# Two upper-part buffers instead of four at the end of the dense block, two expert loads moved ahead, router by contiguous feature blocks, gather in two halves

## The chip, the core and the metric

The program runs on one core of one Trainium2 chip. The metric is the device time of one execution in microseconds (us), as a median over runs. TensorE is called PE, VectorE DVE, ScalarE ACT, GpSimd POOL, and SyncE SP; SP issues nearly all transfers from the chip's memory (HBM).

## What is computed

Two transformer blocks over 256 tokens of width 1024, all in float32.

```python
# first block: stick-breaking attention and a short convolution, then a mixture of experts
h = rms_norm(x, norm_mix_g); proj = h @ w_in            # 1024 x 5120
x = x + (sigmoid(g_a) * branch_a + sigmoid(g_b) * branch_b) @ w_out
h2 = rms_norm(x, norm_ffn_g)
g_logits = h2 @ w_rg + b_rg                             # 4 groups, the best one is taken
e_logits = h2 @ w_re + b_re                             # 8 experts in it, the best two
for each expert e of 32:  y += (silu(h2 @ w_gate[e]) * (h2 @ w_up[e]) * combine[:, e]) @ w_down[e]
x = x + y
# second block: attention and a spatial gating unit, layer norm, SwiGLU of width 2816, layer norm
```

The 32 experts hold 96 MiB of the weights. All of them are read, whatever the router says.

## The kernel before

**Weights.** Every weight comes in units of 1 MiB, 128 partitions by 2048 floats. There is a ring of 12 unit buffers (`ring`). The first block's dense part has 28 units (`B1_UNITS`, numbers 0 to 27), of which the first 20 (`B1_PROJ`) are `w_in`. The experts are worked in 8 quads of four experts, each with 12 units: 4 of gate, 4 of up, 4 of down.

**Dense units.** A float32 product is made of three matmuls from an upper and a lower part of each operand (`mm3`, L656 to L658). For each unit i, ACT copies the landed unit to an upper part `w_hi` (`hi(i)`, recorded as L1303) after waiting for its landing and for the release of the buffer that it writes; DVE subtracts to get the lower part (`lo(i)`, L1767), which takes the place in SBUF of the ring buffer itself; then PE multiplies and adds one to `unit_used`. There are `WB = 4` buffers of `w_hi`, so `hi(i)` waits for unit i - 4. ACT and DVE run strictly in the order in which the kernel writes their work. Units 20 to 23 are the two branch projections in "feature" form (48 matmuls), 24 to 27 are `w_out` in "token" form (24 matmuls of 512 columns). Between them DVE forms the merged activations by halves h: `merge_a(h)` (L1910), `merge_b(h)` (L1915), `merge_sum(h)` (L1921), and after ACT's upper copy `merge_lower(h)` (L1926). Its order there is

```python
merge_a(0); lo(23); merge_b(0); merge_sum(0); lo(24); merge_lower(0)
merge_a(1); merge_b(1); lo(25); merge_sum(1); merge_lower(1); lo(26); lo(27)
```

Each `merge_a` and `merge_b` frees a pair of PSUM banks (`pair_free`). A unit waits for its pair: unit 22 for `merge_a(0)`, unit 23 for `merge_b(0)`, unit 24 for `merge_a(1)`, unit 25 for `merge_b(1)`.

**Early expert loads.** Expert units 0 to 7 and 19 to 23 go to ring buffers as dense units free them (one each from `unit_used` 17 on; unit 3 goes elsewhere, below). Eleven expert units (8 to 18, `EARLY`) go to other memory as it falls free (`EARLY_AT`: place, and the `unit_used` at which it is free). Places 0 to 3 are the four `w_hi` buffers, 4 to 7 the activations of the dense part, `early_a`, `early_b` and `early_c` are elsewhere. Unit 3 has a place `early_d`. So 24 units, those of quads 0 and 1, can be loaded before the first expert matmul; the 25th needs a buffer that quad 0 has used. SP issues all of this from one queue in written order (`early_unit`, L482/L485) and waits in it.

**Router.** DVE adds the last projection to X (`x_add(t, h)`, L1943: token tile t, half h of the features). PE transposes X in 128x128 blocks (L715), taking every eighth feature, DVE or ACT copies the result to `h2T`, and PE multiplies by the router weights `wr` (`router_logits`, L848). DVE forms the choice and the place of each token (L2006 to L2031) and the selection matrix `pick` (L2037).

**A quad.** PE gathers the selected tokens with matmuls by `pick` (`gather`, L902): features 0 to 5 of 8 first, each as upper and lower part for two token tiles, 24 matmuls; features 6 and 7 come after the first gate unit. DVE scales the first four features to `heT` (`gathered(q, s)`, half 0, L2052), then the last four (half 1). PE multiplies the gate units 0 to 3 and the up units 4 to 7 (L936; units 0 and 1 need half 0, units 2 and 3 need half 1), then the down units (L956) and spreads the result to token order (L964, L966). Each unit adds one to the semaphore that SP waits for.

Of the kernel before, what the change touches and what calls it, by code (L numbers as in the profile page):

```python
# [92 lines left out]
def build(nc, consts, x, norm_mix_g, w_in, q_norm_g, k_norm_g, conv_w, w_sb_branch, w_conv_branch, w_out,  # L93
# [3 lines left out]
    with ExitStack() as ctx:  # L97
# [112 lines left out]
        bsp = gain[:, 74:82]  # L210

# [209 lines left out]
        def quad_slot(u):  # L421
# [5 lines left out]
        EARLY_AT = [(early_a, 0), (4, B1_PROJ), (5, B1_PROJ), (6, B1_UNITS - 4), (7, B1_UNITS - 4),  # L427
                    (0, B1_UNITS - 3), (1, B1_UNITS - 2), (2, B1_UNITS - 1), (3, B1_UNITS), (early_b, 0), (early_c, 0)]
        assert len(EARLY_AT) == EARLY

# [16 lines left out]
        def _(sp):  # L447
            def small(dst, src, landed):
                sp.dma_start(dst, src).then_inc(landed, 16)
# [5 lines left out]
            for i, src in enumerate(units1):  # L455
# [11 lines left out]
                if i == RING - 1:  # L467
# [6 lines left out]
                    small(wr[:, :, 0:NG], w_router_group[0].rearrange("(p k) n -> p k n", k=KD), land_small)  # L474
                    small(wr[:, :, NG:NG + NE], w_router_expert[0].rearrange("(p k) n -> p k n", k=KD), land_small)
# [30 lines left out]
            for m in range(RING):  # L506
                if m == GU - 4:
                    early_unit(GU + 1)
                    early_unit(GU + 2)
                if m == GU:  # L510
                    early_unit(GU + 3)
                    early_unit(GU + 4)
                sp.wait_ge(unit_used, B1_UNITS + m - RING + 1)
                n = ring_units[m]
                quad_unit(n // UPQ, n % UPQ, ring[:, QS[m], :], main_sems[m])
                if m >= GU:
                    early_unit(GU + 5 + m - GU)
# [133 lines left out]
        def _(pe):  # L651
# [8 lines left out]
            def parts_of(i, k):  # L660

                slot, _ = slot_of(load_of(i))
                return (w_hi[:, i % WB, :].rearrange("p (k n) -> p k n", k=k),
# [187 lines left out]

            pe.wait_ge(mgT_made, 2)
            for h in range(2):
                pe.wait_ge(lo_made, 27 + h)
                hi, lo = parts_of(26 + h, KU)
                for t in range(T):
                    tok = slice(t * P, (t + 1) * P)
                    for kk in range(KU):
                        last = mm3(ps[:, 2 * h + t, :], mgT_hi[:, KU + kk, tok], mgT_lo[:, KU + kk, tok], hi[:, kk, :],
                                   lo[:, kk, :], start=False, stop=(kk == KU - 1))  # L860
                        if (h, t, kk) == (1, 1, 1):
                            transposes(X, 4, [(x2_made, 3)], (0,))
# [4 lines left out]
            transposes(X, 4, [(x2_made, 3)], (1,))  # L867
            router_logits(0, 1)
            router_logits(1, 0)
# [47 lines left out]
            def quad_hidden(it, s, weights, landed, waits=False):  # L917
# [3 lines left out]
                gather(range(0, 6), s, waits)  # L921
# [370 lines left out]
        def _(act):  # L1292
# [21 lines left out]
            def hi(i):  # L1314
# [3 lines left out]
                if i >= WB:  # L1318
                    act.wait_ge(unit_used, i - WB + 1)
                copy(w_hi[:, i % WB, :], ring[:, slot, :]).then_inc(hi_made, 1)  # L1320
# [163 lines left out]

            for t in range(T):
                act.wait_ge(x2_made, t + 3)
                step(nc.scalar.activation(junk2[:], X[:, t, :], ACT.Square, accum_out=ss2[:, t:t + 1]))
                if t == 1:
                    act.wait_ge(turned_ps, PS_R + 3)
                    copy(h2T[:, 0:4, P:SEQ], ps[:, 6, :].rearrange("p (k n) -> p k n", k=4)).then_inc(h2a_made, 1)  # L1490
                rsqrt(y2[:, t:t + 1], ss2[:, t:t + 1], D, RMS_EPS)
                copy(xs_hi[:, t], X[:, t, :].rearrange("p (q k) -> p k q", k=KD)).then_inc(xshi_made, 1)
# [234 lines left out]
        def _(dve):  # L1727
# [35 lines left out]
            def lo(i):  # L1763
# [3 lines left out]
                tt(w_lo[slot][:], ring[:, slot, :], f32(w_hi[:, i % WB, :]), ALU.subtract).then_inc(lo_made, 1)  # L1767
# [178 lines left out]
            def h2_turned(t, j):  # L1946
                k0 = 4 * j
                dve.wait_ge(turned_ps, PS_R + 2 * t + j + 1)
# [4 lines left out]
            x_add(1, 0)  # L1953
            x_add(0, 1)
            dve.wait_ge(land_small, 16 * 8)
            h2_turned(0, 0)
            h2_turned(0, 1)
            x_add(1, 1)
            refine(y2[:, 0:1], ss2[:, 0:1], D, RMS_EPS)
            h2_turned(1, 1)  # L1960
# [3 lines left out]
            refine(y2[:, 1:2], ss2[:, 1:2], D, RMS_EPS)  # L1964
# [31 lines left out]
            step(ts(margin, margin, float(np.finfo(np.float32).tiny), None, ALU.mult))  # L1996

# [79 lines left out]

            step(tt(emask, oh2, egrp, ALU.mult))
# [3 lines left out]
            gathered(0, start0, (0,))  # L2082
# [319 lines left out]
        def _(pool):  # L2402
# [29 lines left out]
            pool.wait_ge(land_small, 16 * 8)  # L2432
# [50 lines left out]
```

## Time and profile before

| | |
|---|---|
| median of 3 runs | 716.45 us (715.24, 716.45, 718.52) |
| the profiled execution: device time | 715.94 us |
| the profiled execution: span, first to last instruction | 714.1 us |
| PE busy | 650.1 us, 91% of the span |
| DVE busy, ACT busy, POOL busy | 333.6 us, 260.5 us, 30.4 us |
| moved | 186.06 MB, 261 GB/s over the span |
| mean granted clock of TensorE | 0.959 |

A view gives starts and durations in us from the span's start. The page divides the span in 40 slices of 17.85 us; each digit is a busy share in tenths, PEclk the granted clock in tenths, GB/s what the transfers moved. A line number is that of the kernel; "x3" is a row of three like instructions in succession, with the time from the first one's start to the last one's end.

### The profile page before, as it was taken

To read this page: it belongs to the slowest core of one execution; us is meant where nothing else is said; L and a number is where in the kernel's file an instruction comes from. 1 tells how busy PE (TensorE), PEld (TensorE's weight loads), DVE (VectorE), ACT (ScalarE), POOL (GpSimd) and SP (SyncE) were. 2 spreads that over 40 slices of the span, in tenths; PEclk is the share of its full clock that TensorE was granted. 3 is DMA by queue.
4 is the path that set the end of the run, shared out by engine and by line. 5 is a ranking of instruction groups with operands and counts; after the bars stand their busy time and mean duration, and the time that the engine had idled before them with its cause. 6 is when DMAs were issued, how large, how long until landed. Compare 5 with 4: busy or idle time off the path is not lost.

```text
span 714.1 us, 11499 instructions
## 1 busy us (share of the span) xinstructions
PE 650.1 (91%) x4957; PEld 530.3 (74%) x4957; DVE 333.6 (47%) x409; ACT 260.5 (36%) x323; POOL 30.4 (4%) x19
## 2 busy tenths in 40 slices
PE   6999999999989999669787899999899999999995
PEld 5789999999856555244432587778689999999994
DVE  5864437566461222001010465759846444444446
ACT  5747454453411111101010453766236443333330
POOL 0610000000100000000000000330000000000000
PEclk9999999999999999957977899999999999999998
DMA  8979334787999999999999998335445556750001
GB/s 316 408 205 357 121 130 167 253 304 262 406 382 406 386 406 408 409 406 406 409 409 407 389 407 315 116 106 189 143 152 177 177 182 191 259 193 0 0 1 60
DMA packets 108491, 186.06 MB, mean 261 GB/s; under 512 B 9632, under 2 KB 33312, under 8 KB 108448
## 3 DMA queue, kind: packets, MB, share of 16 engines
q1 hardware_dynamic: 108160, 185.36, 70.8%
q8 instruction: 34, 0.56, 0.3%
q10 hardware_dynamic: 288, 0.07, 0.0%
q14 instruction: 9, 0.07, 0.0%
HBM read 184.37 MB, written 1.05 MB: 260 GB/s over the span
## 4 chain that ended last, share of the span: by engine, by line
PE 74%; DMA 11%; DVE 10%; ACT 2%; issue 2%; SPq 1%; DVEq 0%; ACTq 0%
PE ps L656 18%; PE ps L658 17%; PE ps L657 17%; PE ps L936 6%; DMA ring<-in_w_up_e 5%; DMA ring<-in_w_down_e 4%; PE ps L956 4%; PE ps L902 3%; DVE w_lo L1767 3%; DMA ring<-in_w_in 1%; PE ps L964 1%; PE ps L966 1%; PE ps L785 1%; ACT w_hi L1303 1%; DVE X L2314 1%
## 5 line engine op out<-in xcount | busy, mean ns | idle before, releaser
L1303 ACT ACTIVATE w_hi<-ring 128x2048 fp32r<-128x2048 f32 (+1 forms) x77 | 141.1, 1859 | 5.4 <-DMA ring<-in_w_in 5.2
L1767 DVE TENSOR_TENSOR w_lo<-ring,w_hi 128x2048 fp32r<-128x2048 f32 x49 | 114.8, 2354 | 52.2 <-ACT w_hi L1303 52.1
L656 PE MATMUL ps<-xT_hi,w_hi 128*128 128x256 f32 x320 | 90.6, 283 | 0.0
L658 PE MATMUL ps<-xT_hi,w_lo 128*128 128x256 f32 x320 | 90.6, 283 | 0.0
L657 PE MATMUL ps<-xT_lo,w_hi 128*128 128x256 f32 x320 | 90.6, 283 | 0.0
L936 PE MATMUL ps<-ring,heT 128*32 128x256 f32 x880 | 59.0, 409 | 15.6 <-DMA ring<-in_w_up_e 11.0
L656 PE MATMUL ps<-hT_hi,w_hi 128*128 128x256 f32 x224 | 64.0, 286 | 0.0
L657 PE MATMUL ps<-hT_lo,w_hi 128*128 128x256 f32 x224 | 63.4, 283 | 0.0
L658 PE MATMUL ps<-hT_hi,w_lo 128*128 128x256 f32 x224 | 63.3, 283 | 0.0
L657 PEld LDWEIGHTS ps<-xT_lo,w_hi 128*128 128x128 f32 x320 | 61.4, 192 | 0.4
L656 PEld LDWEIGHTS ps<-xT_hi,w_hi 128*128 128x128 f32 x320 | 61.4, 192 | 0.4
L658 PEld LDWEIGHTS ps<-xT_hi,w_lo 128*128 128x128 f32 x320 | 61.4, 192 | 0.0
L2345 DVE TENSOR_TENSOR w_lo<-ring,w_hi 128x2048 fp32r<-128x2048 f32 x24 | 54.3, 2286 | 8.9 <-ACT w_hi L1303 8.9
L936 PEld LDWEIGHTS ps<-ring,heT 128*32 128x32 f32 x880 | 29.1, 115 | 35.9 <-DMA ring<-in_w_up_e 16.2
L656 PE MATMUL ps<-w_hi,xT_hi 128*128 128x512 f32 (+1 forms) x112 | 43.1, 385 | 5.5 <-DVE xT_lo L2161 2.6
L656 PEld LDWEIGHTS ps<-hT_hi,w_hi 128*128 128x128 f32 x224 | 43.0, 192 | 0.2 <-issue 0.2
L657 PEld LDWEIGHTS ps<-hT_lo,w_hi 128*128 128x128 f32 x224 | 43.0, 192 | 0.0
L658 PEld LDWEIGHTS ps<-hT_hi,w_lo 128*128 128x128 f32 x224 | 42.9, 192 | 0.0
L658 PE MATMUL ps<-w_hi,xT_lo 128*128 128x512 f32 (+1 forms) x112 | 41.7, 372 | 0.0
L657 PE MATMUL ps<-w_lo,xT_hi 128*128 128x512 f32 (+1 forms) x112 | 41.5, 370 | 0.0
L956 PE MATMUL ps<-ring,actT 128*32 128x512 f32 x208 | 30.2, 702 | 8.5 <-DMA ring<-in_w_down_e 5.6
L2052 DVE TENSOR_TENSOR heT<-ps,gain 128x512 f32<-128x512 f32 x16 | 11.1, 691 | 53.2 <-PE ps L902 53.0
(315 smaller groups left out, 1128.5 us busy)
## 6 DMA issues: line engine op xcount, KB each, us to landing
ring<-in_w_in SPq DMA_DIRECT2D x29, 1024.0 KB, 13.7
ring<-in_w_up_e SPq DMA_DIRECT2D x28, 1024.0 KB, 13.4
ring<-in_w_gate_e SPq DMA_DIRECT2D x27, 1024.0 KB, 12.4
ring<-in_w_down_e SPq DMA_DIRECT2D x26, 1024.0 KB, 13.4
ring<-in_w_gate SPq DMA_DIRECT2D x11, 1024.0 KB, 5.4
ring<-in_w_up SPq DMA_DIRECT2D x11, 1024.0 KB, 5.5
ring<-in_w_down SPq DMA_DIRECT2D x11, 1024.0 KB, 5.0
ring<-in_w_out SPq DMA_DIRECT2D x8, 1024.0 KB, 9.8
```

The source lines that it names most:

```text
L656: mm(o, a_hi, b_hi, start=start, stop=False, skip_group_check=True)
L657: mm(o, a_hi, b_lo, start=False, stop=False, skip_group_check=True)
L658: return mm(o, a_lo, b_hi, start=False, stop=stop, skip_group_check=True)
L785: mm(o[:, 0:SEQ], negu, stick[:, h, 0:SEQ], start=False, stop=False, skip_group_check=True)
L902: last = mm(ps[:, 6 + k // 4, (k % 4) * P:(k % 4 + 1) * P], xs_lo(t, k) if part else xs_hi[:, t, k, :], pick[:, t, :], start=(part == 0 an ...
L936: last = mm(ps[32 * j:32 * j + 32, 4 + u // 4, 0:FE], heT[:, k, 32 * j:32 * j + 32], wv[:, j // 2, j % 2, kk, :], start=(k == 0), stop=(k ...
L956: last = mm(ps[32 * j:32 * j + 32, 6 + h, :], actT[:, k, 32 * j:32 * j + 32], wv[:, j, :], start=(k == 0), stop=(k == KF - 1))
L964: mm(ps[:, 2 * t + h, :], pickT[:, t, :], ysb_hi[:, cols], start=False, stop=False, skip_group_check=True)
L1303: return nc.scalar.activation(o, i, ACT.Copy)
L1767: tt(w_lo[slot][:], ring[:, slot, :], f32(w_hi[:, i % WB, :]), ALU.subtract).then_inc(lo_made, 1)
L2052: tt(heT[:, 4 * b:4 * b + 4, :], ps[:, 6 + b, :].rearrange("p (k n) -> p k n", k=4), bc(g2[:, 4 * b:4 * b + 4], P), ALU.mult).then_inc(s[" ...
L2345: tt(w_lo[slot][:], ring[:, slot, :], f32(w_hi[:, i % WB, :]), ALU.subtract).then_inc(lo_made, 1)
```

## The change

Units 20 to 27 use only `w_hi` buffers 0 and 1, in turn, so that buffers 2 and 3 take expert loads from `unit_used` 20 on. Four early loads are then issued from `unit_used` 20 on, in place of two (the third and fourth ahead of the next two ring loads); with `unit_used` 25 and 26 there is none any more, where one each was. The router's features go in contiguous blocks of 128 (k p) in place of every eighth, so its transposes can be done by halves of X as each half is added; its weights and a second copy of the gain (`g2_block`) are loaded in that layout. The first quad's `heT` half 0 is moved ahead of four small DVE steps, and the first gather call (features 0 to 5) becomes two (0 to 3, then 4 and 5).

```diff
-        EARLY_AT = [(early_a, 0), (4, B1_PROJ), (5, B1_PROJ), (6, B1_UNITS - 4), (7, B1_UNITS - 4),
-                    (0, B1_UNITS - 3), (1, B1_UNITS - 2), (2, B1_UNITS - 1), (3, B1_UNITS), (early_b, 0), (early_c, 0)]
+        EARLY_AT = [(early_a, 0), (2, B1_PROJ), (3, B1_PROJ), (4, B1_PROJ), (5, B1_PROJ),
+                    (6, B1_UNITS - 4), (7, B1_UNITS - 4), (0, B1_UNITS - 1), (1, B1_UNITS), (early_b, 0), (early_c, 0)]
+        def upper_of(i):
+            return i % 2 if B1_PROJ <= i < B1_UNITS else i % WB
+        upper_user = {}
+        for i in range(S1 + B2_PRE + 2):
+            upper_user[i] = max((j for j in range(i) if upper_of(j) == upper_of(i)), default=None)
...
-                    small(wr[:, :, 0:NG], w_router_group[0].rearrange("(p k) n -> p k n", k=KD), land_small)
-                    small(wr[:, :, NG:NG + NE], w_router_expert[0].rearrange("(p k) n -> p k n", k=KD), land_small)
+                    with nc.allow_non_contiguous_dma(reason="router weights by blocks of features"):
+                        small(g2_block, norm_ffn_g[0].rearrange("(k p) -> p k", p=P), land_small)
+                        small(wr[:, :, 0:NG], w_router_group[0].rearrange("(k p) n -> p k n", p=P), land_small)
+                        small(wr[:, :, NG:NG + NE], w_router_expert[0].rearrange("(k p) n -> p k n", p=P), land_small)
...
             for m in range(RING):
-                if m == GU - 4:
-                    early_unit(GU + 1)
-                    early_unit(GU + 2)
-                if m == GU:
-                    early_unit(GU + 3)
-                    early_unit(GU + 4)
+                for k in {GU - 4: (1, 2), GU - 3: (3,), GU - 2: (4,), GU: (5, 6)}.get(m, ()):
+                    early_unit(GU + k)
                 sp.wait_ge(unit_used, B1_UNITS + m - RING + 1)
...
-                if m >= GU:
+                if m >= GU + 2:
                     early_unit(GU + 5 + m - GU)
...
+            def router_turn(t, j):
+                pe.wait_ge(x2_made, 1 + t + 2 * j)
+                for k in range(4 * j, 4 * j + 4):
+                    ins = nc.tensor.transpose(ps[:, 4 + 2 * t + j, (k % 4) * P:(k % 4 + 1) * P],
+                                              X[:, t, k * P:(k + 1) * P], ident)
+                ins.then_inc(turned_ps, 1)
...
+                        if (h, t, kk) == (1, 0, 2):
+                            router_turn(0, 0)
+                            router_turn(1, 0)
                         if (h, t, kk) == (1, 1, 1):
-                            transposes(X, 4, [(x2_made, 3)], (0,))
+                            router_turn(0, 1)
...
             router_logits(0, 0)
-            transposes(X, 4, [(x2_made, 3)], (1,))
             router_logits(0, 1)
+            router_turn(1, 1)
             router_logits(1, 0)
             router_logits(1, 1).then_inc(logit_ps, 1)
...
-                gather(range(0, 6), s, waits)
+                gather(range(0, KD // 2), s, waits)
+                gather(range(KD // 2, 6), s, waits)
...
             def hi(i):
-                if i >= WB:
-                    act.wait_ge(unit_used, i - WB + 1)
-                copy(w_hi[:, i % WB, :], ring[:, slot, :]).then_inc(hi_made, 1)
+                before = upper_user.get(i, i - WB)
+                if before is not None:
+                    act.wait_ge(unit_used, before + 1)
+                copy(w_hi[:, upper_of(i), :], ring[:, slot, :]).then_inc(hi_made, 1)
...
+            act.wait_ge(turned_ps, PS_R + 2)
+            copy(h2T[:, 0:4, P:SEQ], ps[:, 6, :].rearrange("p (k n) -> p k n", k=4)).then_inc(h2a_made, 1)
             for t in range(T):
                 act.wait_ge(x2_made, t + 3)
                 step(nc.scalar.activation(junk2[:], X[:, t, :], ACT.Square, accum_out=ss2[:, t:t + 1]))
-                if t == 1:
-                    act.wait_ge(turned_ps, PS_R + 3)
-                    copy(h2T[:, 0:4, P:SEQ], ps[:, 6, :].rearrange("p (k n) -> p k n", k=4)).then_inc(h2a_made, 1)
                 rsqrt(y2[:, t:t + 1], ss2[:, t:t + 1], D, RMS_EPS)
-                copy(xs_hi[:, t], X[:, t, :].rearrange("p (q k) -> p k q", k=KD)).then_inc(xshi_made, 1)
+                if t == 0:
+                    xs_upper(0, slice(0, KD // 2))
+            xs_upper(0, slice(KD // 2, KD)).then_inc(xshi_made, 1)
+            xs_upper(1, slice(0, KD)).then_inc(xshi_made, 1)
...
             x_add(0, 0)
             x_add(1, 0)
+            h2_turned(0, 0)
             x_add(0, 1)
-            dve.wait_ge(land_small, 16 * 8)
-            h2_turned(0, 0)
             h2_turned(0, 1)
+            dve.wait_ge(land_small, 16 * 9)
+            refine(y2[:, 0:1], ss2[:, 0:1], D, RMS_EPS)
             x_add(1, 1)
-            refine(y2[:, 0:1], ss2[:, 0:1], D, RMS_EPS)
-            h2_turned(1, 1)
...
+            gathered(0, start0, (0,))
             step(tt(emask, oh2, egrp, ALU.mult))
             ts(oh1, rank, 0.0, None, ALU.is_equal)
             step(red(m2, emask, AX, ALU.add))
             tt(eexp, m2, m1, ALU.subtract).then_inc(gdiff_made, 1)
-            gathered(0, start0, (0,))
```

`h2_turned(1, 1)` and the second `refine` move behind two small DVE steps that need neither. PE's, ACT's and DVE's indices into `w_hi` all go through `upper_of`.

## Rows read from the trace of the kernel before

**Rows 1.** The page's 40 slices: PE, granted clock, GB/s.

```profile
PE   6999999999989999669787899999899999999995
...
PEclk9999999999999999957977899999999999999998
...
GB/s 316 408 205 357 121 130 167 253 304 262 406 382 406 386 406 408 409 406 406 409 409 407 389 407 315 116 106 189 143 152 177 177 182 191 259 193 0 0 1 60
```

**Rows 2.** The chain that ended last, 240 to 470 us: start, duration, what.

```profile
371.05 16.32 DMA ring<-in_w_up_e
387.40 1.98 PE ps L936 x16
```

**Rows 3.** Stretches: busy time (and instructions) by engine, granted clock, DMA share, GB/s.

```profile
165.00:170.00 5.00, 5.00 (x39) 4.79 (x38) 0.95 (x1) 0.00 (x0) 0.00 (x0) 1.00 0.50 191
...
175.00:180.00 5.00, 5.00 (x24) 4.14 (x23) 4.42 (x3) 3.31 (x2) 0.00 (x0) 1.00 1.05 408
...
232.50:235.00 2.50, 1.81 (x16) 0.74 (x18) 0.91 (x3) 0.66 (x2) 0.00 (x0) 1.00 1.00 333
```

**Rows 4.** SP's queue in order of time: start, duration, line, transfer, count.

```profile
146.41 1.05 SPq L485 DMA_DIRECT2D early<-in_w_down_e  x2
151.76 17.65 SPq L482 DMA_DIRECT2D ring<-in_w_up_e  x4
169.45 0.51 SPq L485 DMA_DIRECT2D early<-in_w_down_e  x1
...
174.92 0.51 SPq L482 DMA_DIRECT2D early<-in_w_gate_e  x1
...
191.76 0.37 SPq L485 DMA_DIRECT2D ring<-in_w_down_e  x1
...
202.92 0.37 SPq L482 DMA_DIRECT2D early_c<-in_w_up_e  x1
...
218.96 4.93 SPq L485 DMA_DIRECT2D early<-in_w_down_e  x2
232.41 3.02 SPq L485 DMA_DIRECT2D ring<-in_w_down_e  x2
```

**Rows 5.** ACT, DVE and PE around unit 24, in order of time.

```profile
150.14 5.53 ACT L1303 ACTIVATE w_hi<-ring 128x2048 fp32r<-128x2048 f32 x3
...
160.09 2.29 DVE L1767 TENSOR_TENSOR w_lo<-ring,w_hi 128x2048 fp32r<-128x2048 f32 x1
162.30 1.22 DVE L1926 TENSOR_TENSOR mgT_lo<-ga,mgT_hi 128x1024 fp32r<-128x1024 f32 x1
163.43 1.22 DVE L1910 TENSOR_TENSOR ga<-ps,ga 128x1024 f32<-128x1024 f32 x1
...
168.85 0.40 PE L656 MATMUL ps<-w_hi,mgT_hi 128*128 128x512 f32 x1
```

**Rows 6.** PE from the router's transposes of tile 1 to its last logits.

```profile
192.51 1.16 PE L715 MATMUL ps<-cst,X 128*128 128x128 f32 x8
193.51 2.79 PE L848 MATMUL ps<-wr,h2T 128*128 128x36 f32 x24
```

**Rows 7.** DVE around quad 0's start; the chain at quad 1's start.

```profile
201.70 1.13 DVE L2076 TENSOR_TENSOR xs_lo1b<-X,xs_hi 128x512 fp32r<-128x512 f32 x1
...
203.51 0.69 DVE L2052 TENSOR_TENSOR heT<-ps,gain 128x512 f32<-128x512 f32 x1
...
206.45 0.69 DVE L2052 TENSOR_TENSOR heT<-ps,gain 128x512 f32<-128x512 f32 x1
...
223.31 0.60 issue
```

**Rows 8.** SP's small loads at 33 us, the loads behind them, ACT's upper copy of unit 12.

```profile
32.78 6.12 SPq L449 DMA_DIRECT2D gain<-in_b_spatial  x1
...
44.81 17.93 SPq L460 DMA_DIRECT2D ring<-in_w_in  x8
...
84.11 1.90 ACT L1303 ACTIVATE w_hi<-ring 128x2048 fp32r<-128x2048 f32 x1
```

More of the change, by code:

```diff
@@ L210, in build @@
         bsp = gain[:, 74:82]
+        g2_block = gain[:, 82:90]
         ss1, y1, n1 = st[:, 0:2], st[:, 2:4], st[:, 4:10]
@@ L662, in parts_of @@
                 slot, _ = slot_of(load_of(i))
-                return (w_hi[:, i % WB, :].rearrange("p (k n) -> p k n", k=k),
+                return (w_hi[:, upper_of(i), :].rearrange("p (k n) -> p k n", k=k),
                         w_lo[slot][:].rearrange("p (k n) -> p k n", k=k))
@@ L1482, in _, with xs_upper @@
             hi(27)
+            act.wait_ge(turned_ps, PS_R + 2)
+            copy(h2T[:, 0:4, P:SEQ], ps[:, 6, :].rearrange("p (k n) -> p k n", k=4)).then_inc(h2a_made, 1)
+            def xs_upper(t, ks):
+                return copy(xs_hi[:, t, ks], X[:, t, :].rearrange("p (q k) -> p k q", k=KD)[:, ks])
             for t in range(T):
@@ L1766, in lo @@
                 dve.wait_ge(hi_made, i + 1)
-                tt(w_lo[slot][:], ring[:, slot, :], f32(w_hi[:, i % WB, :]), ALU.subtract).then_inc(lo_made, 1)
+                tt(w_lo[slot][:], ring[:, slot, :], f32(w_hi[:, upper_of(i), :]), ALU.subtract).then_inc(lo_made, 1)
             def bc(ap, n):
@@ L1947, in h2_turned @@
                 k0 = 4 * j
-                dve.wait_ge(turned_ps, PS_R + 2 * t + j + 1)
+                dve.wait_ge(turned_ps, PS_R + t + 2 * j + 1)
                 nc.vector.tensor_copy(h2T[:, k0:k0 + 4, t * P:(t + 1) * P],
@@ L1963, in _ @@
                 nc.vector.engine_nop().then_inc(pair_free[h], 1)
-            refine(y2[:, 1:2], ss2[:, 1:2], D, RMS_EPS)
             pos = [0]
@@ L1996, in _ @@
             step(ts(margin, margin, float(np.finfo(np.float32).tiny), None, ALU.mult))
+            h2_turned(1, 1)
+            refine(y2[:, 1:2], ss2[:, 1:2], D, RMS_EPS)
             def beats(out, vals, n):
@@ L2428, in _ @@
                    ).then_inc(normed_split, 1)
-            pool.wait_ge(land_small, 16 * 8)
-            tt(wr[:], wr[:], g2.unsqueeze(2).to_broadcast([P, KD, NG + NE]), ALU.mult).then_inc(wr_made, 1)
+            pool.wait_ge(land_small, 16 * 9)
+            tt(wr[:], wr[:], g2_block.unsqueeze(2).to_broadcast([P, KD, NG + NE]), ALU.mult).then_inc(wr_made, 1)
             def xs_lower(t, parts):
```

## The prediction

> **What bounds the kernel now.** I began with the page's slices [rows 1]. PE is at nine tenths nearly everywhere but in the 17th to the 23rd slice (286 to 411 us), and exactly there the transfers stand at 389 to 409 GB/s. From the 11th to the 24th they never fall below 382. So three regimes follow each other: a dense part paced by PE, an expert part paced by the weight stream, and a second block paced by PE again, where the rate is 106 to 259 GB/s, with nothing to load at the very end. The chain of waits gives the seam: PE waits 16.32 us for an expert unit's landing and starts at 387.40 [rows 2]; what follows in the chain is computation. What decides the end is when the stream delivers the last expert units, and that is the moment from which it runs without a hole, plus the bytes left. One unit is 1.0486 MB, 2.57 us at 408 GB/s.
>
> Then the stretches and SP's queue, to see where the stream is short of bytes and where of buffers. At 165 to 170 us it moves 191 GB/s, at 175 to 180 it moves 408 [rows 3]. SP issues ring loads as PE finishes dense units: four between 151.76 and 169.41, that is at 151.76, 157.5, 163.3 and 169.04, 5.76 us apart, for `unit_used` 21 to 24 [rows 4]. Two early loads follow at 169.45, and from 174.51 on each of three ring loads brings one early load along (that of 174.92 is shown), so nine loads are issued from 169.04 until just before 191.76. At 2.57 us that is 23.1 us of work in 22.7 us: just busy. The last free buffers are filled by the loads issued at 218.96 to 223.89; then SP issues nothing until 232.41, when quad 1 gives back a ring buffer, and the rate at 232.5 to 235 falls to 333 GB/s [rows 3, 4]. **This is the point on which I build:** at 232 us the stream has run out of buffers, not of time. Whatever moves earlier before it is lost in this gap, unless PE gives the buffer back earlier.
>
> **The two loads moved ahead.** No buffer is added; 24 units can still be in place before quad 0. Of those issued at 174.92 and about 5.4 us later, two transfers (5.14 us of stream) go into the hole of 152 to 169 us. Issued from 169.04 to 191.76 are then seven loads, 18.0 us of work: the stream idles nearly 5 us there. After 191.76 the same loads follow as before. What can reach 232 us is no more than the backlog that stood at 191.76: 23.1 - 22.7 = 0.4 us from below, one load of 2.57 us from above, since the time from issue to first byte is open. I take 0.7 us, near the lower end, up to there, and 0 beyond it, because the gap before 232.41 takes it.
>
> **Two upper buffers.** `hi(i)` now waits for unit i - 2. Durations are those of [rows 5]: three `hi` in 5.53 us, 1.84 us apart and 1.90 long (the single one in [rows 8]), `lo` 2.29 (2.21 to the next start), merges 1.22 (1.13). By the release times of [rows 4]: `hi(22)` starts at 151.76, `lo(22)` ends at 156.0, `merge_a(0)` at 157.1; unit 22 would start at 157.3, no loss. `hi(23)` starts at 157.5, `lo(23)` ends 161.7, `merge_b(0)` 162.9; unit 23 would start at 163.1, no loss. `hi(24)` waits for unit 22, released at 163.3, and ends at 165.2. `lo(24)` runs to 167.5, where before it ran at 160.09. Behind it in DVE's order stand `merge_lower(0)`, to 168.7, and `merge_a(1)`, to 169.8. Unit 24 needs all three, the last for its PSUM pair; before, it started at 168.85. **PE stalls 1.0 us there.** Next: `lo(25)` ends about 173.2 against unit 25's start, now near 175.3; `hi(26)` may start at 175.5 and `lo(26)` ends at 179.7 against 180.7; `lo(27)` ends near 185.1 against 186.2. None of these is late. Bounds: 0 (if the stall were covered) to 1.2 us (one more merge).
>
> **Small loads.** The three new small loads take 1024 pieces each (g2 in 4 bytes, the weights in rows of 16 and 128 bytes). The nearest row is the load of `b_spatial`, also 1024 pieces of 4 bytes: 6.12 us on SP's queue [rows 8]. From below they cost what single rows cost now, under 1 us each; from above 3 x 6.12 = 18.4 us. Queued behind them are the ring loads from 44.81 on, unit 12 first, which ACT needs at 84.11. Even 18.4 us later it is issued at 63.2, 21 us ahead. The cost is 0; with that cover gone it would be up to 18 us. The Trainium skill ("DMA: Bandwidth & Descriptors", Rules for kernel authors) says that a strided last dimension lowers to one descriptor per element, and advises against it. It speaks against this edit; the row of `b_spatial` agrees that such a load is slow, and by either the sum stays the same, since the cover is wider than the price.
>
> **Router.** PE is the bound from the last dense matmul to the logits: 8 transposes, then 24 router instructions with no idle between [rows 6]. The change moves transposes but makes as many (16): four more fall inside unit 27 (0.1 us each, from 8 in about 1.0 us, so it ends 0.4 us later) and four fewer behind it. Net 0; I take -0.1 us for the shorter wait on the last copy. ACT's copies to `xs_hi` end about 1 us later, POOL's lower part about 3 us later, at 198.5; the gather needs it after 202, so both are covered by 3 us.
>
> **Gather.** `heT` half 0 becomes possible after 16 matmuls, not 22. At 0.11 us each that is 0.7 us earlier. In quad 0 DVE is free only when `xs_lo1b` is done, 201.70 + 1.13 = 202.83, so half 0 moves from 203.51 to 202.8: -0.7. But the four small steps now stand behind it, ACT's exponential waits for them, and all DVE work up to half 1 goes with it: half 1, before at 206.45, comes 0.2 us later [rows 7]. Gate unit 2 needs half 1 at 207.1 already. So the gain of units 0 and 1 ends in a wait for half 1: quad 0 as a whole +0.2 us. Bounds: -0.7 (half 1 not late) to +0.3. In quad 1 the idle 0.60 us before the first gate matmul [rows 7] goes, because the 8 matmuls of features 4 and 5 run beside DVE's 0.69: -0.6 us, bounds -0.6 and 0.
>
> **Sum.** The release that comes at 232.41 shifts by +1.0 (stall) - 0.1 (router) + 0.2 (quad 0) - 0.6 (quad 1) = +0.5 us. The stream restarts 0.5 us later, runs at the same rate over the same bytes, and hands over at 387.9 in place of 387.4; behind it nothing changes. The profiled execution has 715.94 us, 1.8 above its span of 714.1, and lies 0.5 under the median of the three runs. 715.94 + 0.5 = 716.4; set to the median, 716.45 + 0.5, about 716.9. Ends of the terms: 0 - 0.1 - 0.7 - 0.6 = -1.4 and 1.2 + 0.3 = +1.5; with the runs' own spread (715.24 to 718.52) the likeliest case has the range 715 to 718.6.
>
> **Rivals.** *No stall* (chance 0.17). If `merge_a(1)` or `lo(24)` is not late, the sum is -0.5 or, with half 1 in time, down to -1.4: 715.1 to 716.0. For it: the slack in the dense part is large elsewhere. Against it: DVE's written order.
>
> *The two loads count in full* (0.13). If the gap at 232 is not a shortage of buffers but a side effect of the full queue, so that bytes moved before stay moved, the stream ends 2 x 2.57 = 5.1 us earlier: 711.3. For it: 400 GB/s from 171 us on, so every byte in it seems to cost. Against it: SP's 8.5 us without an issue. The Trainium skill (same page and section) advises to issue a transfer early, so that it overlaps computation. By that rule alone this rival would be the result; the rule doesn't ask whether a buffer is free later on.
>
> *Slower* (0.10). The two buffers put release, `hi` and `lo` in series: 0 + 1.9 + 2.3 = 4.2 us in units of 5.45 to 5.76. If in units 24 to 27 each `lo` also had a 1.22 us merge in front of it that my order of events puts elsewhere, three more stalls of 1.0 to 1.2 follow: +0.5 + 3.4 = +3.9, 720.4. It decides once the stalls pass 4.1 us in all; each passes one to one to the release at 232.41. Against it: 1.0 us or more of slack at each of units 25 to 27 above.
>
> **Chances.** Forecast 0.60, no stall 0.17, both within 0.5%, which is 3.6 us and about what a measurement of this kernel can tell from no change; full gain 0.13, faster; slower 0.10. That gives faster 0.13, same 0.77, slower 0.10. The range of 8 in 10 holds the first two with their spread and reaches toward both others: 712.5 to 719.5.
>
> **What would show it.** Right: one PE idle of about 1.0 us before the first matmul of unit 24, ended by L1910 of DVE; GB/s higher in 152 to 169 us and well under 400 in 175 to 192; SP's first ring load after quad 1's release at 232 to 233.5; the 0.60 us idle gone in each quad; quad 0 waiting for half 1 of `heT`; the stretch behind the last expert landing as long as before. Wrong: the stream's rate not falling around 233, or the landing at 387.4 moved by over 2 us; several idles in units 24 to 27; or a different spell of lowered clock behind 387 us, which I haven't priced.

## The result, and the profile after

The changed kernel takes 718.51 us (median of 12 runs, 715.44 to 723.84), the kernel before beside it 717.07 (12 runs, 714.03 to 719.03). The ratio is 1.0042 with an interval of 1.0022 to 1.0063, so some 3.0 us slower (1.6 to 4.5). Forecast were 0.5 us more. A second measurement of the same two kernels (e10, below) gave 1.0020 [0.9996, 1.0044], 1.4 us (-0.3 to 3.2). All medians and ratios are of fast runs; one run of the kernel before, taken beside e13, was slow (1264.35 us) and is not counted. The profiled execution took 720.63 us with a span of 718.8 and a mean granted clock of 0.946, against 0.959 before.

The page's slices answer to [rows 1]:

```profile
PE   6999999999999999769777898999899999999995
...
PEclk9999999999999999768887699999999999999998
...
GB/s 316 408 158 393 127 132 169 251 337 346 271 346 406 398 407 408 409 406 407 409 409 408 398 408 293 118 71 222 121 172 176 176 176 182 253 207 1 0 1 59
```

The regimes are the same: from the 13th to the 24th slice the transfers stand at 398 to 409 GB/s. New is the 11th slice (180 to 198 us), 271 where [rows 1] have 406. In the chain of waits the landing that releases the second block ends 1.8 us later, at 389.18 where it was 387.37 [rows 2]:

```profile
375.34 13.84 DMA ring<-in_w_up_e
389.23 1.98 PE ps L954 x16
```

SP's queue, beside [rows 4]:

```profile
146.32 0.37 SPq L493 DMA_DIRECT2D ring<-in_w_up_e  x1
...
157.84 0.37 SPq L493 DMA_DIRECT2D ring<-in_w_up_e  x1
158.25 0.51 SPq L493 DMA_DIRECT2D early<-in_w_gate_e  x1
163.62 6.11 SPq L493 DMA_DIRECT2D ring<-in_w_up_e  x2
169.78 1.06 SPq L493 DMA_DIRECT2D early<-in_w_gate_e  x2
...
235.00 3.02 SPq L496 DMA_DIRECT2D ring<-in_w_down_e  x2
```

In before the first of these rows reads:

```profile
146.00 0.37 SPq L482 DMA_DIRECT2D ring<-in_w_up_e  x1
```

I count from this row, the ring load issued when unit 20 is done, because runs differ by up to 1.1 us in this row, runs of one kernel too (146.32 and 145.32 for the changed one). From it to the first ring load after quad 1's release (the last row of the queue shown; "the release" below) are 232.41 - 146.00 = 86.41 us before and 88.68 after. This **distance to the release** is 2.27 us longer; the forecast was 0.5. It is the measure for all runs below, since the prediction rests on the release passing one to one to the end.

The stretches of 5 us, with the columns of [rows 3]:

```profile
155.00:160.00 5.00, 5.00 (x44) 5.00 (x43) 2.67 (x3) 1.91 (x1) 0.00 (x0) 1.00 1.05 409
160.00:165.00 5.00, 5.00 (x44) 5.00 (x44) 4.50 (x3) 1.31 (x1) 0.00 (x0) 1.00 1.05 406
...
185.00:190.00 5.00, 5.00 (x28) 4.24 (x27) 2.67 (x4) 0.14 (x1) 0.00 (x0) 1.00 0.58 189
```

In before, 155 to 165 us moved 315 and 173 GB/s, and 185 to 190 moved 409. The moved loads fill the hole and leave another behind it, as forecast.

DVE and PE around unit 24, beside [rows 5]:

```profile
165.64 2.29 DVE L1792 TENSOR_TENSOR w_lo<-ring,w_hi 128x2048 fp32r<-128x2048 f32 x1 [1.03 <-ACT w_hi L1321]
167.85 1.22 DVE L1951 TENSOR_TENSOR mgT_lo<-ga,mgT_hi 128x1024 fp32r<-128x1024 f32 x1
168.98 1.22 DVE L1935 TENSOR_TENSOR ga<-ps,ga 128x1024 f32<-128x1024 f32 x1
...
169.06 0.28 PE L665 MATMUL ps<-brT_hi,w_lo 128*128 128x256 f32 x1
170.30 0.47 PE L663 MATMUL ps<-w_hi,mgT_hi 128*128 128x512 f32 x1 [0.96 <-issue]
```

The reader is to see three DVE operations end to end, `lo(24)`, `merge_lower(0)`, `merge_a(1)`, and PE starting unit 24 at 170.30, 0.1 us after the last one's end, with 0.96 us of idle before it. That is the stall, where it was put.

Now the place that the prediction passed over. First POOL and DVE before, then after, around the first two routing steps behind the logits:

```profile
192.63 2.87 POOL L2440 TENSOR_TENSOR xs_lo<-X,xs_hi 128x1024 fp32r<-128x1024 f32 x1 [142.77 <-ACT xs_hi L1303]
...
196.41 0.42 DVE L2006 SCALAR_TENSOR_TENSOR rt<-ps,st,gain 128x36 f32<-128x36 f32 x2 [0.58 <-PE ps L848]
196.86 0.19 DVE L2000 TENSOR_TENSOR rt<-rt 128x32 f32<-128x32 f32 x1
...
200.32 0.42 DVE L2037 TENSOR_TENSOR pick<-cst,rt 128x256 fp32r<-128x256 f32 x1
```

```profile
192.81 1.16 ACT L1321 ACTIVATE xs_hi<-X 128x512 fp32r<-128x512 f32 x1
...
196.09 3.11 ACT L1321 ACTIVATE xs_hi<-X 128x512 fp32r<-128x512 f32 x2
...
197.28 2.86 POOL L2465 TENSOR_TENSOR xs_lo<-X,xs_hi 128x1024 fp32r<-128x1024 f32 x1 [144.92 <-ACT xs_hi L1321]
...
198.38 0.42 DVE L2031 SCALAR_TENSOR_TENSOR rt<-ps,st,gain 128x36 f32<-128x36 f32 x2 [1.06 <-PE ps L855]
198.83 1.36 DVE L2025 TENSOR_TENSOR rt<-rt 128x32 f32<-128x32 f32 x1
200.22 0.19 DVE L2027 TENSOR_TENSOR rt<-rt 128x32 f32<-128x32 f32 x1
...
203.45 0.43 DVE L2062 TENSOR_TENSOR pick<-cst,rt 128x256 fp32r<-128x256 f32 x1
```

The same subtraction of 128x32 numbers takes 0.19 us in before and 1.36 after, and ends at 200.19, when POOL's ends (200.14). ACT now copies the upper part of tile 0 in two halves, the second behind the square and root of tile 1, so POOL's lower part starts at 197.28 and runs beside DVE's routing. No row of a wait shows this: the time is booked as DVE's busy time.

Quad 0, beside [rows 7]:

```profile
205.97 0.69 DVE L2077 TENSOR_TENSOR heT<-ps,gain 128x512 f32<-128x512 f32 x1
...
209.73 0.68 DVE L2077 TENSOR_TENSOR heT<-ps,gain 128x512 f32<-128x512 f32 x1
...
210.47 1.07 PE L954 MATMUL ps<-ring,heT 128*32 128x256 f32 x16 [0.60 <-DVE heT L2077]
```

From `pick` to half 1 are 6.28 us, where before they were 206.45 - 200.32 = 6.13; PE waits for half 1 as forecast. Half 0 itself comes 2.52 us after `pick`, before 3.19: 0.67 earlier, as forecast.

### The profile page after: what moved, and what is told of

It is laid out like the page before. It is cut to its first block, busy times and chain, and to the rows that moved or that the text cites. A ratio compares the mean times of both kernels' runs of the same rounds, so it can differ in the third digit from the quotient of the medians.

```text
span 718.8 us, 11501 instructions
## 1 busy us (share of the span) xinstructions
PE 658.1 (92%) x4957; PEld 532.9 (74%) x4957; DVE 335.3 (47%) x409; ACT 261.3 (36%) x324; POOL 30.4 (4%) x19
## 3 DMA queue, kind: packets, MB, share of 16 engines
HBM read 184.37 MB, written 1.05 MB: 258 GB/s over the span
## 4 chain that ended last, share of the span: by engine, by line
PE 73%; DVE 11%; DMA 11%; ACT 2%; issue 2%; SPq 1%; DVEq 0%; ACTq 0%
PE ps L663 18%; PE ps L665 17%; PE ps L664 17%; DMA ring<-in_w_up_e 6%; PE ps L954 5%; PE ps L974 4%; DMA ring<-in_w_down_e 4%; PE ps L919 3%; DVE w_lo L1792 3%; DMA ring<-in_w_in 1%; PE ps L982 1%; PE ps L984 1%; PE ps L855 1%; PE ps L792 1%; SPq L493 1%
## 5 line engine op out<-in xcount | busy, mean ns | idle before, releaser
L954 PE MATMUL ps<-ring,heT 128*32 128x256 f32 x880 | 62.7, 425 | 12.9 <-DMA ring<-in_w_up_e 11.9
L2083 DVE SCALAR_TENSOR_TENSOR act_e<-ps,st,sil 128x256 f32<-128x256 f32 x8 | 3.9, 484 | 66.9 <-PE ps L954 66.9
## 6 DMA issues: line engine op xcount, KB each, us to landing
ring<-in_w_down_e SPq DMA_DIRECT2D x26, 1024.0 KB, 13.6
```

What stands on the lines that cost most here:

```text
L954: last = mm(ps[32 * j:32 * j + 32, 4 + u // 4, 0:FE], heT[:, k, 32 * j:32 * j + 32], wv[:, j // 2, j % 2, kk, :], start=(k == 0), stop=(k ...
```

## The experiments

All kernels were timed beside the kernel before, with 12 runs each, save e13 (6) and e7 (one). The medians of the kernel before differ between the measurements: 717.07 us beside the changed kernel, 716.30 beside e1 to e3, 716.54 beside e5, e6, e8 and e9, 716.60 beside e10 to e12, 717.06 beside e13. The ratio is to these, so times are compared by ratio, not by median. The other columns are of each kernel's one profiled run. "DVE" is the first routing subtraction.

| kernel | median us | ratio [interval] | 20th unit's load | release | distance | against before | DVE us |
|---|---|---|---|---|---|---|---|
| before | 717.07 | | 146.00 | 232.41 | 86.41 | | 0.19 |
| changed | 718.51 | 1.0042 [1.0022, 1.0063] | 146.32 | 235.00 | 88.68 | +2.27 | 1.36 |
| e1 | 717.39 | 1.0036 [1.0007, 1.0066] | 145.43 | 232.89 | 87.46 | +1.05 | 1.80 |
| e2 | 717.11 | 1.0013 [0.9991, 1.0036] | 145.35 | 232.97 | 87.62 | +1.21 | 0.19 |
| e3 | 715.86 | 0.9991 [0.9968, 1.0013] | 146.06 | 231.59 | 85.53 | -0.88 | 0.19 |
| e5 | 717.27 | 0.9995 [0.9969, 1.0021] | 146.29 | 234.25 | 87.96 | +1.55 | 0.19 |
| e6 | 714.51 | 0.9976 [0.9949, 1.0003] | 145.22 | 231.29 | 86.07 | -0.34 | 0.19 |
| e7 | 725.99 | one run | 145.55 | 242.38 | 96.83 | +10.42 | 1.80 |
| e8 | 716.48 | 0.9990 [0.9968, 1.0013] | 146.00 | 231.76 | 85.76 | -0.65 | 0.19 |
| e9 | 716.78 | 1.0001 [0.9976, 1.0027] | 146.16 | 232.82 | 86.66 | +0.25 | 0.19 |
| e10 | 717.77 | 1.0020 [0.9996, 1.0044] | 145.32 | 233.99 | 88.67 | +2.26 | 1.80 |
| e11 | 717.18 | 1.0001 [0.9977, 1.0025] | 145.53 | 232.48 | 86.95 | +0.54 | 0.19 |
| e12 | 716.86 | 1.0001 [0.9979, 1.0023] | 145.98 | 232.76 | 86.78 | +0.37 | 0.19 |
| e13 | 722.39 | 1.0093 [1.0062, 1.0124] | 145.97 | 240.64 | 94.67 | +8.26 | 2.68 |

No kernel tried is faster than the one before by more than its interval.

The distance has three parts in every run: from the 20th unit's load to the first routing step ("to the logits", 50.41 us in the kernel before), from there to `pick` (3.91) and from `pick` to the release (32.09). Against these:

| kernel | to the logits | routing | behind `pick` | sum |
|---|---|---|---|---|
| changed | +1.65 | +1.16 | -0.54 | +2.27 |
| e1 | -0.02 | +1.61 | -0.54 | +1.05 |
| e2 | +1.21 | 0.00 | 0.00 | +1.21 |
| e3 | 0.00 | 0.00 | -0.88 | -0.88 |
| e5 | +1.17 | +0.91 | -0.53 | +1.55 |
| e6 | +0.19 | 0.00 | -0.53 | -0.34 |
| e7 | +1.20 | +3.94 | +5.28 | +10.42 |
| e8 | +0.21 | 0.00 | -0.86 | -0.65 |
| e9 | +0.24 | 0.00 | +0.01 | +0.25 |
| e10 | +1.18 | +1.60 | -0.52 | +2.26 |
| e11 | +0.17 | +0.92 | -0.55 | +0.54 |
| e12 | -0.02 | +0.91 | -0.52 | +0.37 |
| e13 | -0.01 | +2.48 | +5.79 | +8.26 |

**e1, four upper buffers.** The changed kernel with the old buffers, and with the old `EARLY_AT` and order of early loads (those lines are left out here):

```diff
-            return i % 2 if B1_PROJ <= i < B1_UNITS else i % WB
+            return i % WB
```

> The changed kernel with the dense part as before: four upper buffers and the old places and times of the early loads; the router and the gather stay changed. Theory (stalls passed on): the idle of about 1 us before unit 24 goes, SP's ring load for the 28th dense unit comes 1.2 us earlier than in the changed kernel (about 192.5 in place of 193.76), the first expert release likewise, and the time is about 1.2 us below the changed kernel's and still 1 to 2 us above the kernel before. Rival A (the time is lost behind 387 us, in a spell of lowered clock that has nothing to do with the dense part): no difference from the changed kernel. Rival B (the router part costs nothing, the buffers cost all): the time of the kernel before.

The distance shrinks by 1.22 us, the stall's size, and 1.05 us remain that the buffers have no part in: 1.61 in the routing, less 0.54 behind `pick`. The time doesn't show the gain of 1.2 us that was expected (1.0036 against 1.0042). Its runs had a mean clock of 0.956, those of the kernel before beside them 0.962.

**e2, the buffers and early loads alone,** put into the kernel before.

> The kernel before with the two upper buffers and the moved early loads alone; router and gather as before. Theory: unit 24 starts 1.2 us late, logits and the release that came at 232.4 us are 1.2 us late too, and the time is 1 to 1.5 us above the kernel before. Rival (the bytes moved earlier count): the last expert landing, before at 387.4 us, comes earlier in spite of the stall, up to 5.1 - 1.2 = 3.9 us.

+1.21 us, the stall again, and DVE's subtraction takes 0.19. The last landing in the chain, counted from the 20th unit's load, comes 0.21 us later than before (386.93 - 145.35 against 387.37 - 146.00), not up to 3.9 us earlier, as bytes that stay moved would have it.

**e3, the gather in two halves alone,** in the kernel before:

```diff
-                gather(range(0, 6), s, waits)
+                gather(range(0, KD // 2), s, waits)
+                gather(range(KD // 2, 6), s, waits)
```

> The kernel before with the first gather call split in two (features 0 to 3, then 4 and 5), nothing else. Theory: the 0.60 us idle before the first gate matmul goes from quad 1 on, in quad 0 next to nothing changes (DVE is free only at 203.4), the release at 232.4 comes 0.6 to 0.7 us earlier, and the time is 0.5 us lower, not to be told from no change. Rival (the gap at 232 us is not set by the release): the last expert landing stays at 387.4.

-0.88 us at the release, somewhat more than expected; in the time no difference that can be told. The landing, counted likewise, comes 1.44 us earlier (385.99 - 146.06), so the rival is out: it doesn't stay.

**e7, POOL's subtraction twice,** in the changed kernel; the first one's result is written over by the second. It asks whether POOL's work costs DVE time.

```diff
+            again = sem("again")
+            pool.wait_ge(xshi_made, 1)
+            tt(xs_lo0[:], X[:, 0, :].rearrange("p (q k) -> p k q", k=KD), xs_hi[:, 0].bitcast(F32), ALU.subtract).then_inc(again, 1)
+            pool.wait_ge(again, 1)
             xs_lower(0, ((xs_lo0, slice(0, KD)),))
```

> The changed kernel, in which POOL computes the lower part of token tile 0 twice in a row (the same values), so that it is busy 2.9 us longer from 197.3 us on. Theory (a DVE subtraction of two SBUF operands cannot run beside POOL's tensor operation and waits for its end): the DVE operation at L2025, 1.36 us in the changed kernel against 0.19 us before, gets longer still or the next one does, by up to 2.9 us in all, and the selection matrix comes that much later. Rival (that operation was long for another reason): it takes 1.36 or 0.19 us and DVE's chain does not move.

POOL's and DVE's rows of this run:

```profile
196.50 2.87 POOL L2470 TENSOR_TENSOR xs_lo<-X,xs_hi 128x1024 fp32r<-128x1024 f32 x1 [145.06 <-ACT xs_hi L1321]
199.44 2.91 POOL L2465 TENSOR_TENSOR xs_lo<-X,xs_hi 128x1024 fp32r<-128x1024 f32 x1
...
197.62 1.80 DVE L2025 TENSOR_TENSOR rt<-rt 128x32 f32<-128x32 f32 x1
199.45 0.19 DVE L2027 TENSOR_TENSOR rt<-rt 128x32 f32<-128x32 f32 x1
199.68 0.19 DVE L2035 TENSOR_REDUCE rt<-rt 128x8 f32<-128x32 f32 x1
199.90 2.60 DVE L2037 SCALAR_TENSOR_TENSOR rt<-rt 128x32 f32<-128x32 f32 x2
```

The first long operation ends at 199.42, with POOL's first (199.37). Then an equal subtraction and a reduction pass at 0.19 beside POOL's second, and the next pair with two operands in SBUF takes 2.60 in place of 0.29 and ends at 202.50, with POOL's (202.35). ACT's copies end at 198.4 here and at 199.20 in the changed kernel, about 1 us before the long subtraction does, so they are not what it waits for. So DVE waits for POOL, and which operation waits is not settled by its form alone: the one at 199.45 began 0.01 us behind POOL's second and was not held. On DVE 1.61 and 2.31 us are lost, 3.9 in all and 2.8 more than in the changed kernel (1.17), but the release comes 8.15 us later than there. The other part lies behind `pick`, where PE has the lower clock (see e13).

**e5, the upper part of tile 0 whole,** in the changed kernel, so that POOL is done before the routing:

```diff
                 if t == 0:
-                    xs_upper(0, slice(0, KD // 2))
-            xs_upper(0, slice(KD // 2, KD)).then_inc(xshi_made, 1)
+                    xs_upper(0, slice(0, KD)).then_inc(xshi_made, 1)
```

> The changed kernel, in which ACT copies the upper part of token tile 0 whole before it squares tile 1 (as before the change), in place of half before and half after. Theory (DVE waits for POOL): POOL's subtraction starts about 1 us earlier against the logits, so DVE's first router subtraction takes 0.2 to 0.7 us in place of 1.4 to 1.8, the selection matrix comes 1.1 to 1.6 us earlier against the logits, the release after the 232 us gap likewise; the time is 1 to 1.5 us below the changed kernel's. Rival (the wait only moves to the next operation, or the squares of tile 1, now later, hold the logits up as much): no gain.

```profile
194.92 2.86 POOL L2464 TENSOR_TENSOR xs_lo<-X,xs_hi 128x1024 fp32r<-128x1024 f32 x1 [142.39 <-ACT xs_hi L1321]
...
198.32 0.19 DVE L2024 TENSOR_TENSOR rt<-rt 128x32 f32<-128x32 f32 x1
```

POOL ends at 197.78 and DVE's subtraction is back at 0.19, but the distance shrinks by 0.72 us only. The rest is lost to another wait in the same routing. Between the logits and the first placement matmul PE works on six products of X, and a spell of lowered clock lies over them (0.50 from 198 to 201 us). DVE and PE in e5, then the same products in e6:

```profile
197.59 4.52 PE L890 MATMUL ps<-X,cst 128*128 128x512 f32 x6
...
202.34 0.23 DVE L2053 SCALAR_TENSOR_TENSOR rt<-ps,asg 128x64 f32<-128x64 f32 x1 [0.95 <-PE ps L901]
```

```profile
195.55 2.82 PE L890 MATMUL ps<-X,cst 128*128 128x512 f32 x6
```

In e5 PE finishes them at 202 and DVE waits 0.95 us for PE; in e6, at full clock, DVE doesn't wait there, and the whole routing takes 3.91 us as before. e11 and e12 have e5's spell and e5's loss (+0.92, +0.91). So the held subtraction is best priced between runs without the spell: 5.51 us of routing in e10 against 3.91 in e6, 1.60 us.

**e6 and e11, both places mended** (the same kernel in two measurements): the whole upper part as in e5, and the merge ahead of `lo(24)`:

```diff
             merge_sum(0)
+            merge_a(1)
             lo(24)
             merge_lower(0)
-            merge_a(1)
```

> The changed kernel with two orders mended: merge_a(1) ahead of lo(24) in DVE's order, and the upper part of token tile 0 copied whole. Theory: the idle before unit 24 falls from 1.0 us to 0.3 or less, DVE's wait for POOL to 0.7 or less; the release comes 0.5 us earlier than in the kernel before (counted from the 20th dense unit), the last expert landing 1 to 1.5 us earlier, and the time is 1 us below the kernel before. Rival (loads moved ahead are worth nothing, as I predicted): the last landing moves only as the release does, the time is that of the kernel before.

> The kernel with both orders mended once more: 1 us below the kernel before at an equal clock, 2.3 us below the changed kernel, if the first measurement (-1.7 us) was not chance.

The distance falls to -0.34 and +0.54 against before; what lies between the two is the spell described under e5. The first time (714.51, ratio 0.9976) looked like a gain; the second (717.18, 1.0001) did not, so the gain of 1 us that was expected isn't shown.

**e9, e2 with that merge ahead of `lo(24)`, and e8, the same with the gather in two halves.**

> The kernel before with the two upper buffers and the moved loads, and merge_a(1) ahead of lo(24); router and gather as before. It prices the moved loads alone. Theory now: release as before within 0.3 us, last expert landing 0.7 to 1.0 us earlier (counted from the 20th dense unit), time 0.8 us lower. Rival 1 (my prediction: the gap at 232 us takes all): landing as before. Rival 2 (bytes moved stay moved): landing 5.1 us earlier.

> The kernel before with the two upper buffers, the moved loads, merge_a(1) ahead of lo(24), and the gather in two calls; the router as before. Theory: no stall, no wait for POOL, release 0.6 to 0.9 us earlier, last expert landing 1.5 to 2.4 us earlier than in the kernel before (counted from the 20th dense unit), time 2 us lower: about 0.3%. Rival: the landing moves as the release does, 0.9 us.

e9 has +0.25 us where e2 had +1.21: the stall is that one merge behind `lo(24)`, and the two early loads, kept in this kernel, are worth nothing at the release. In the time they are not to be told from nothing either, and the interval (0.9976 to 1.0027) leaves no room for the rival's 5.1 us, a ratio of 0.993. The landing that was to be compared isn't in e9's chain. With the gather's split -0.65: it gives 0.90, as in e3 (0.88). e8's landing comes 1.07 us earlier than before, not 1.5 to 2.4, and the time is 0.7 us lower and not 2, which can't be told from no change.

**e10, the changed kernel again.**

> The changed kernel once more, beside the two below on one chip. At an equal mean clock it should lie 1.2 to 1.5 us above the kernel before, which is the shift of its last expert landings. Theory C1 (part of the measured 3 us is clock that the change itself costs, by its idles near 197 to 203 us): its median clock is again 0.005 or more below that of the kernels without the wait for POOL. Theory C2 (that part was chance of the first measurement): its clock is like theirs, and the time is 1.5 us above the kernel before.

```profile
196.25 2.87 POOL L2465 TENSOR_TENSOR xs_lo<-X,xs_hi 128x1024 fp32r<-128x1024 f32 x1 [144.75 <-ACT xs_hi L1321]
...
197.36 1.80 DVE L2025 TENSOR_TENSOR rt<-rt 128x32 f32<-128x32 f32 x1
```

The distance is the same to 0.01 us. The time is 1.4 us over before, not 3.0, and the median clock is 0.962 where e11's and e12's are 0.956 and 0.957: that speaks for C2 and against C1. PE stood idle in this run too, for 2.21 us, while DVE was held:

```profile
201.67 0.19 PE L897 MATMUL ps<-asg,ltri_b 128*128 128x32 bf16 x1 [2.21 <-DVE asg L2045]
```

The granted clock stayed at 1.00 from 190 to 222 us.

**e12, e1 with the whole upper part of e5.** What is left of the change is the router and the gather.

> The changed kernel with four upper buffers and the old early loads, and the upper part of token tile 0 copied whole: router and gather of the change without stall and with a shorter wait for POOL. Theory (moved loads are worth nothing): the stream after the gap at 232 us, counted from the 20th dense unit, stands where that of the mended kernel does or 0.3 us earlier; the time equals the mended one's. Rival (moved loads are worth something): it comes at least 1 us after the mended one's.

DVE's subtraction goes from 1.80 to 0.19 us, the distance from +1.05 to +0.37; the other 0.91 us are the wait for PE described under e5. The time equals e11's (both 1.0001), and the release stands between e6's and e11's and not 1 us behind them, so the rival is out.

**e13, POOL's subtraction late in the kernel before,** with no part of the change in it: ACT copies both upper parts only after tile 1's root.

```diff
-                copy(xs_hi[:, t], X[:, t, :].rearrange("p (q k) -> p k q", k=KD)).then_inc(xshi_made, 1)
+                if t == 1:
+                    for u in range(T):
+                        copy(xs_hi[:, u], X[:, u, :].rearrange("p (q k) -> p k q", k=KD)).then_inc(xshi_made, 1)
```

> The kernel before, in which ACT copies the upper part of token tile 0 only after the square and root of tile 1; nothing of the change is in it. POOL's subtraction, which waits for that copy, then runs from about 194.6 to 197.5 us, over the first DVE subtraction of two SBUF operands behind the logits (L2000 at 196.86 before). Theory (DVE waits there until POOL is done): that operation takes 0.6 to 1.8 us in place of 0.19, the selection matrix and the release at 232 us come 0.5 to 1.6 us later, and so does the stream behind it. Rival (the long operation belongs to another part of the change): it stays at 0.19 us and nothing moves.

POOL, DVE and PE, then the stretches behind them:

```profile
196.59 2.87 POOL L2442 TENSOR_TENSOR xs_lo<-X,xs_hi 128x1024 fp32r<-128x1024 f32 x1 [145.74 <-ACT xs_hi L1303]
...
196.82 2.68 DVE L2002 TENSOR_TENSOR rt<-rt 128x32 f32<-128x32 f32 x1
199.54 0.19 DVE L2004 TENSOR_TENSOR rt<-rt 128x32 f32<-128x32 f32 x1
...
202.00 0.19 PE L880 MATMUL ps<-asg,ltri_b 128*128 128x32 bf16 x1 [3.09 <-DVE asg L2022]
```

```profile
205.00:210.00 5.00, 4.60 (x29) 4.04 (x33) 2.30 (x14) 1.49 (x2) 0.00 (x0) 0.50 0.62 216
210.00:216.00 6.00, 6.00 (x52) 3.43 (x45) 2.18 (x11) 0.00 (x0) 0.00 (x0) 0.50 0.54 177
```

An operation of 0.19 us takes 2.68, and moving POOL's work alone makes the kernel before 6.6 us slower (ratio 1.0093, 4.4 to 8.9 us). The release was expected 0.5 to 1.6 us later. `pick` comes only 2.4 us later (202.76 against 200.32), the release 8.26. Before `pick` PE stood idle for 3.09 us, and behind that the granted clock was 0.50 in the two stretches shown, 1.2 GHz, where the kernel before has 1.00 from 205 to 210 us. In e7, whose PE was busy for 0.77 us of 200 to 205, the clock is 0.50 too from 205 to 216. That the idle brings the clock down is read from these two runs and e10's; no run moves the idle alone.

## Why the prediction was wrong

**The step that failed** is in the router's part: "POOL's lower part about 3 us later, at 198.5 ... covered by 3 us". The delay was foreseen and nearly right: in e1, without the stall, POOL's end is 3.1 us later than before, counted from the 20th unit's load (198.02 - 145.43 against 195.50 - 146.00). Wrong was the question put to it. By the forecast's own figure POOL would have worked from 195.6 to 198.5, across the subtraction that stood at 196.86. I asked who needs POOL's result, which is the gather after 202, and not what runs on DVE while POOL runs. So a wait was put at nothing. Its price is the extra time of one subtraction: 1.36 - 0.19 = 1.17 us in the profiled run, 1.80 - 0.19 = 1.61 in e10. e5 and e12 take it away by ACT's order alone, and so POOL's start, e6 and e11 together with the merge, e7 adds to it, and e13 makes it in a kernel with nothing of the change. The Trainium skill has the rule for it ("SBUF — State Buffer", SBUF: two separate sides): a DVE operation with two SBUF inputs and a GpSimd operation that reads SBUF take the same ports by an exclusive lock, and the second to come is blocked to the end of the first. The traces agree for the long operations, which end within 0.15 us of POOL's. The 0.19 us at 199.45 in e7 shows that not every such operation is caught.

**The bounding point held.** e9 moves two loads ahead and stands at +0.25 us at the release and 1.0001 in the ratio, not at the -5.1 us of the rival. Whether a later release passes "one to one" to the end is shown less sharply. The landing in the chain moved by +1.49 us in the changed kernel (389.18 - 146.32 against 387.37 - 146.00) where the release moved by 2.27, and in e2, e3, e5, e8 and e13 too it stands 0.4 to 1.2 us below what the release would give. Compared with each other these runs agree better: from the changed kernel to e13 the release is 5.99 us later and the landing 5.58. Part of the gap may thus lie in the one profile of the kernel before; that isn't shown. The times can't settle it: 6.6 us (4.4 to 8.9) for 8.26 at the release in e13, 1.4 (-0.3 to 3.2) for 2.26 in e10.

**The stall held,** place, order and size: 1.0 forecast, 0.96 of idle seen, unit 24 starting 1.13 us later, and 1.21 to 1.22 us at the release by e2 and e1, the upper bound of 1.2. e9 gives back 0.96. None of units 25 to 27 stalled, so the slower rival's mechanism did not come; its sign came through another one.

**Router.** Forecast -0.1. In e10 the routing starts 1.18 us later than before, counted from the 20th unit, and the stall alone makes 1.2. The router itself is 0, as e12 shows too (its logits stand at -0.02).

**Gather.** Forecast +0.2 - 0.6 = -0.4, and in the changed kernel -0.54 lie behind `pick` (-0.52 in e10). Half 1 of quad 0 comes 0.15 us later; from there to the release it is 0.69 us less (25.27 against 25.96). Both parts are near the forecast. The -0.88 of e3 is more because there half 0 is not moved ahead of the four small steps: half 1 comes 0.21 us earlier than before, and the rest is the same -0.67. So moving half 0 ahead cost 0.36 us against the split alone. That is read from the rows; no run has the changed router and the old place of half 0.

**Small loads.** Forecast 0; nothing behind them is late. They also took under 1 us each on the queue, where the upper bound was 6.12. Why `b_spatial`, a load of as many pieces, takes 6.13 us in the same queue stays open:

```profile
42.98 0.98 SPq L458 DMA_DIRECT2D gain<-in_norm_ffn_g  x2
44.01 0.58 SPq L458 DMA_DIRECT2D wr<-in_w_router_group  x1
44.63 0.82 SPq L458 DMA_DIRECT2D wr<-in_w_router_expert  x1
```

**The sum** over the release is, in e10, +1.18 (stall and router) + 1.60 (the held subtraction) - 0.52 (gather) = +2.26, and nothing is left over. Against the forecast of +0.5 the miss is 1.76 us, and 1.60 of them are the term put at nothing. The first profiled run has +1.65 + 1.16 - 0.54 = +2.27: there the clock fell at 197 us, PE's last 16 router instructions took 2.53 us and not 2.10 as in e10, so the logits came about 0.45 us later and the subtraction was held for as much less, since POOL ends at the same time in both (53.8 us after the 20th unit's load).

Against the first 3.0 us of time there is another part to explain. The changed kernel's runs there had a median granted clock of 0.9535, those of the kernel before in the later measurements 0.957 to 0.962 (beside the first only that of its profiled run is known, 0.959). Over the runs of one kernel the time falls by about 3.2 us for each 0.01 of mean clock; that makes 1.1 to 2.7 us. In e10 the clock was 0.962, and the difference 1.4 us. By these medians alone the two measurements don't agree. Read at one clock of 0.958 by a straight line through each kernel's runs, the changed kernel stands at 718.1 (718.2 in e10) and before at 716.6 to 716.8: 1.4 us again. So I estimate that some 1.4 us belong to the change, and the rest of the first 3.0 to the clock; no experiment shows it. Read in the same way e6 stands 1.0 us and e11 0.8 us below the kernel before, again as an estimate. Whether the change has a part in that clock stays open: a short spell of lowered clock at 196 to 200 us was in the profiles of the changed kernel, e5, e11 and e12 and not in those of e1, e2, e3, e6, e8, e9, e10 and before, and e11 is the same kernel as e6, e10 the same as the changed one.

Around and behind the last landing the profiled run had 23.9 us at the lower level where before had 13.6 in two pieces (from 383.6 and from 400.2 us on):

```profile
384.60:408.50 23.90, 18.74 (x92) 8.99 (x80) 7.72 (x8) 6.74 (x9) 0.00 (x0) 0.51 1.05 406
```

From the landing to the end the profiled run took 329.6 us, the kernel before 326.7. The prediction named a different spell there as a sign of being wrong and gave it no price.

## What to carry to other kernels

When an instruction is moved to another time, ask two questions: who needs its result, and what runs on the neighbouring engines while it runs. For POOL the second means DVE's operations with two operands in SBUF. Do the same for the path that is freed: in e5 the wait for POOL went, and a wait for PE took more than half of its place. An operation whose mean is right and whose single row is several times longer is a hidden wait; look for it by single rows around the start and end of POOL's work, not in the waits. And bytes moved earlier are worth something only if a buffer is free where the stream next stops.

## What the runs showed of the hardware

- A 128x32 subtraction on DVE, 0.19 us by itself, took 1.36, 1.80 and 2.68 us beside a POOL subtraction of 2.87 us. Operations with a PSUM operand were not held (0.42 us at 198.38 beside POOL, as before). POOL's own time did not change (2.86 to 2.91).
- A wait can cost three times its length: in e13 2.4 us on DVE became 8.26 at the release and 6.6 in the time. PE's idle of 3.09 us was followed by a granted clock of 0.50 until 216 us. In the changed kernel PE's idle at that place was 0.53 us and in e10 2.21 us, and no such long spell followed. A short spell at 0.50 stands in one profile of a kernel (e11) and not in the other (e6); in both PE was busy just before.
- At a granted clock of 0.50 six products of X took 4.52 us of PE, at 1.00 2.82 us.
